# Projection tiles in order of need, earlier first mixers, weight loads on ScalarE's queue

## The reference

```python
# first kind, twice
z = rms_norm(x, g) @ w_in                      # 3612 columns: Fox, conv and NSA parts
o_a = fox_attention(fq, fk, fv, ff + fox_b) * silu(f_gate)
o_b = conformer_conv(glu_in, ...) * silu(c_gate)       # 31 taps, LayerNorm, pointwise
o_c = nsa_attention(nq, nkc, ..., cmp_v_w2) * silu(n_gate)  # compressed, selected, window
x = x + concat(o_a, o_b, o_c) @ w_out
# second kind, twice
z = rmsnorm(x, g1) @ w_in_2                    # gated delta net, differential attention,
                                               # sliding window attention, mLSTM
x = x + (sum over 4 branches of gate_b * (y_b @ w_branch[b])) @ w_out_2
x = x + square(relu(rmsnorm(x, g2) @ w_mlp1)) @ w_mlp2
```

## Time and profile before

| | us |
|---|---|
| median of 3 runs (3993.82 to 4000.56) | 3995.27 |
| the profiled execution | 3999.47 |
| its span, first to last instruction | 3997.7 |
| TensorE busy | 3478.4 (87%) |
| VectorE busy | 2067.8 (52%) |
| ScalarE busy | 1448.1 (36%) |
| GpSimd busy | 396.9 (10%) |

### The profile page before, as it was taken

One profiled execution on the slowest core, in us unless ns is written; L12 is line 12 of the kernel. 1 busy time (PEld: TensorE's weight loads), 2 busy tenths in 40 slices (PEclk: granted clock), 3 DMA queues, 4 the chain that ended last, 5 costly groups with the idle time before them and its releaser, 6 DMA issues. The chain is left out here.

```text
span 3997.7 us, 48121 instructions
## 1 busy us (share of the span) xinstructions
PE 3478.4 (87%) x17580; PEld 2861.8 (72%) x17580; DVE 2067.8 (52%) x4076; ACT 1448.1 (36%) x2809; POOL 396.9 (10%) x322
## 2 busy tenths in 40 slices
PE   7877888779789999779879999889999789689998
PEld 5766867568567888668657888668888577577886
DVE  3474634746328776445553333248875455563333
ACT  2313333134324444334334332225544344334322
POOL 0000000000002223000112111002222000112110
PEclk9987899889899999899979999889999899899999
DMA  4632046330244322422333333343321422433332
GB/s 137 175 96 72 20 115 180 98 75 20 70 129 132 88 82 64 115 65 63 94 93 92 95 95 94 102 120 106 96 79 61 116 70 68 112 90 86 93 95 84
DMA packets 570480, 373.52 MB, mean 93 GB/s; under 512 B 77020, under 2 KB 500956, under 8 KB 569980
## 3 DMA queue, kind: packets, MB, share of 16 engines
q1 hardware_dynamic: 570236, 370.33, 33.6%
HBM read 310.69 MB, written 59.57 MB: 93 GB/s over the span
## 5 line engine op out<-in xcount | busy, mean ns | idle before, releaser
L767 PE MATMUL bank<-h,w_hi 128*128 128x512 f32 x2240 | 974.0, 435 | 170.8 <-DVE w_low L760 91.3
L768 PE MATMUL bank<-h,w_hi 128*128 128x512 f32 x2240 | 913.4, 408 | 0.0
L769 PE MATMUL bank<-h,w_low 128*128 128x512 f32 x2240 | 910.9, 407 | 0.0
L754 ACT CAST w_hi<-w 128x1024 fp32r<-128x1024 f32 (+1 forms) x456 | 432.7, 951 | 699.9 <-DMA w<-in_w_mlp 398.7
L760 DVE TENSOR_TENSOR w_low<-w,w_hi 128x1024 fp32r<-128x1024 f32 (+1 forms) x456 | 514.3, 1128 | 289.2 <-ACT w_hi L754 281.2
L767 PEld LDWEIGHTS bank<-h,w_hi 128*128 128x128 f32 x2240 | 437.8, 195 | 302.5 <-DVE w_low L760 139.0
L769 PEld LDWEIGHTS bank<-h,w_low 128*128 128x128 f32 x2240 | 435.9, 195 | 110.2
L768 PEld LDWEIGHTS bank<-h,w_hi 128*128 128x128 f32 x2240 | 438.6, 196 | 104.3 <-issue 14.9
L768 PE MATMUL bank<-yT_low,w_hi 128*128 128x512 f32 x768 | 312.2, 407 | 0.0
L1423 ACT ACTIVATE prob<-bank,softmax_stat 128x512 f32<-128x512 f32 (+3 forms) x256 | 145.0, 568 | 300.8 <-DVE softmax_stat L1457 211.6
L1226 DVE TENSOR_TENSOR xT<-xT,bank 128x512 f32<-128x512 f32 x80 | 55.0, 687 | 285.4 <-PE bank L769 285.4
(11 more groups left out here) (409 smaller groups left out, 5744.0 us busy)
## 6 DMA issues: line engine op xcount, KB each, us to landing
w<-in_w_in SPq DMA_DIRECT2D x148, 512.0 KB, 4.2
w<-in_w_mlp SPq DMA_DIRECT2D x128, 512.0 KB, 4.0
w<-in_w_gate SPq DMA_DIRECT2D x64, 512.0 KB, 4.2
z<-z_tile SPq DMA_DIRECT2D x110, 256.0 KB, 4.3
w<-in_w_branch SPq DMA_DIRECT2D x64, 256.0 KB, 2.9
z_hi<-row_part_high SPq DMA_DIRECT2D x54, 256.0 KB, 2.0
z<-z_tile_low SPq DMA_DIRECT2D x54, 256.0 KB, 2.3
k_hi<-z_hi SPq DMA_DIRECT2D x36, 256.0 KB, 7.4
```

What stands on the lines that cost most here:

```text
L754: self.a.copy(self.wh[s][:, 0:d, 0:n], self.w[s][:, 0:d, 0:n]).then_inc(self.w_high.sem, 1)
L767: self.t.matmul(bank[0:n, :], wh, high, start=j == 0, stop=False)
L768: self.t.matmul(bank[0:n, :], wh, low, start=False, stop=False)
L769: return self.t.matmul(bank[0:n, :], wl, high, start=False, stop=j == self.depth(i) - 1)
```

## The change

- **Order.** A new function `sequence` gives the z tiles an order of their own; the rows of z in DRAM stay as they were. Layer one: ff first, then one tile each of fq, fk, fv, fg for the first pair of heads, the same for the second, then nq, glu, cg, nkc, nvc, nks, nkw, nvs, nvw, ng. Layer two: a_ab first, then q, k, v, z of each Gdn head in turn; from position 17 on as before. The waits for stored rows name the tile that is needed, head by head, in place of the last of the group.
- **Start.** Both layers go densely to unit 6 only. Layer one: Fox to unit 22, ConvAndCompress to unit 27, and Nsa runs beside the last two z tiles and the first `out` units. Layer two: Gdn to unit 47, and the gates of branch 3 are spread: three ahead of branch 0, two ahead of branch 1, three ahead of branch 2.
- **Pieces.** Fox 0.7 to 1.6 for each step and 2.0 to 4.0 at its end; a tap 0.75 to 0.2; Nsa 3.0 to 9.0 at its start; Gdn's first yield 1.0 to 5.0, 3.0 to 6.0 in head 0, 2.0 to 4.0 ahead of `o_normed`; Diff 2.0 to 6.0 and Mlstm 1.0 to 6.0 ahead of `h_normed`; Swa 0.95 to 1.15 for each step, and 1.0 to 2.0 twice.
- **Loads of the mixers.** Value rows first, then keys, then queries; gains and the like behind them; the rows of the second part as soon as their buffer is free. Semaphores are split to fit. In Gdn the scalars' loads come first. In Nsa the second keys, queries and the gates wait for their own tiles.
- **Weights.** `fetch` takes the engine; the first two loads are SyncE's, all others ScalarE's, ahead of `split_high` of the next unit.

```diff
+def sequence(first, last, groups):
+    order = []
+    for names in groups:
+        rows = [range(first[name] // P, last[name] + 1) for name in names]
+        order += [tile for part in zip(*rows, strict=True) for tile in part]
+    place = {tile: i for i, tile in enumerate(order)}
...
+ORDER1, PLACE1 = sequence(C1, LAST1, (("ff",), ("fq", "fk", "fv", "fg"), ("nq",), ("glu",), ("cg",), ("nkc",), ("nvc",), ("nks",), ("nkw",),
+                                      ("nvs",), ("nvw",), ("ng",)))
+ORDER2, PLACE2 = sequence(C2, LAST2, (("a_ab",), ("a_q", "a_k", "a_v", "a_z"), ("b_q",), ("b_k",), ("b_v",), ("c_q",), ("c_k",), ("c_v",),
+                                      ("d_q",), ("d_k",), ("d_v",), ("d_o",)))
...
-    def fetch(self, i):
+    def fetch(self, eng, i):
...
-                self.s.wait_ge(*self.multiplied(i - self.SLOTS))
+                eng.wait_ge(*self.multiplied(i - self.SLOTS))
...
+        self.units = [("z", 0, e) for e in ORDER2]
+        for s, early in enumerate(((0, 1, 2), (3, 4), (5, 6, 7))):
+            self.units += [("gate", 3, e) for e in early] + pairs[2 * KD * s:2 * KD * (s + 1)]
...
             if self.pieces(i) == 4:
                 yield
+                self.fetch(self.a, i + 2)
                 self.split_high(i + 1)
...
-        yield 3.0
+        yield 9.0
+        self.t.wait_ge(*self.stream.drained(self.stream.kept - 1))
         self.t.wait_ge(*self.gl_in(0))
...
-            stream.go_to(("z", 0, LAST1["fg"] + 2))
-            stream.until(("z", 0, LAST1["nvc"] + 3))
-            Fox(k, l, stream, w1).beside(stream, ("z", 0, LAST1["nvc"] + 2))
-            stream.until(("out", 0, 0))
-            ConvAndCompress(k, l, stream, kcmp, vcmp, table, w1).beside(stream, ("out", 0, 0), stream.forms_out)
+            stream.go_to(stream.units[PLACE1["fg", 0] + 2])
+            stream.until(stream.units[PLACE1["nvc", 0] + 2])
+            Fox(k, l, stream, w1).beside(stream, stream.units[PLACE1["nvc", 0] + 2])
+            stream.until(stream.units[PLACE1["ng", 2]])
+            ConvAndCompress(k, l, stream, kcmp, vcmp, table, w1).beside(stream, stream.units[PLACE1["ng", 2]], stream.forms_out)
...
-        yield 3.0
+        yield 3.0 if h else 6.0
...
+        start, scalars = self.prepare_sp(0), self.scalars_sp()
+        next(scalars)
         next(start)
...
+            yield (1.0 if n else 5.0) if share is None else share
...
+        self.stream.wait_stored(s, PLACE2["b_v", 3])
+        self.fetch_v(0)
+        self.fetch_k(0)
+        self.fetch_q(0)
...
-            yield 1.0
+            yield 6.0
             self.t.wait_ge(*self.h_normed(p))
...
-        stream.go_to(("z", 0, LAST2["a_ab"] + 2))
-        stream.until(("gate", 0, 0))
-        Gdn(k, l, stream).beside(stream, ("gate", 3, 2), stream.forms_out)
+        stream.go_to(stream.units[PLACE2["a_z", 0] + 2])
+        stream.until(("gate", 3, 0))
+        Gdn(k, l, stream).beside(stream, ("gate", 3, 0), stream.forms_out)
...
-    stream.until(("gate", 1, 0))
-    Diff(k, l, stream).beside(stream, ("gate", 1, 0))
-    stream.until(("gate", 2, 0))
-    Swa(k, l, stream).beside(stream, ("gate", 2, 0))
+    stream.until(("gate", 3, 3))
+    Diff(k, l, stream).beside(stream, ("gate", 3, 3))
+    stream.until(("gate", 3, 5))
+    Swa(k, l, stream).beside(stream, ("gate", 3, 5))
```

More of the change, by code:

```diff
@@ L72 @@
                                ("raw", 1.0, [("d_o", 512)])))
+def sequence(first, last, groups):
[4 more added lines that the diff above has]
+    place = {tile: i for i, tile in enumerate(order)}
+    return order, {(name, j): place[first[name] // P + j] for name in first for j in range(last[name] + 1 - first[name] // P)}
+ORDER1, PLACE1 = sequence(C1, LAST1, (("ff",), ("fq", "fk", "fv", "fg"), ("nq",), ("glu",), ("cg",), ("nkc",), ("nvc",), ("nks",), ("nkw",),
+                                      ("nvs",), ("nvw",), ("ng",)))
+ORDER2, PLACE2 = sequence(C2, LAST2, (("a_ab",), ("a_q", "a_k", "a_v", "a_z"), ("b_q",), ("b_k",), ("b_v",), ("c_q",), ("c_k",), ("c_v",),
+                                      ("d_q",), ("d_k",), ("d_v",), ("d_o",)))
 LEVELS = 7
@@ L726, in store_row @@
     def store_row(self, i):
-        if 0 <= i < self.kept:
+        if 0 <= i and self.units[i][0] == "z":
             e, n = self.units[i][2], self.width(i)
@@ L783, in __init__ @@
         self.l = l
-        self.units = [("z", 0, e) for e in range(len(TILES1))] + [("out", s, e) for s in range(2) for e in range(KD)]
+        self.units = [("z", 0, e) for e in ORDER1] + [("out", s, e) for s in range(2) for e in range(KD)]
         self.tiles, self.kept = TILES1, len(TILES1)
@@ L1035, in bank_of, with wait_kept @@
         return self.banks[i % 2]
+    def wait_kept(self, eng, i, last):
+        eng.wait_ge(*self.row_out[i].nth(sum(r % 3 == i and r <= last for r in self.kept_rows) - 1))
     def wait_row_free(self, eng, r):
@@ L1040, in wait_row_free @@
             return
[L1041 to L1044, removed]
+        if r - 3 in self.kept_rows:
+            self.wait_kept(eng, r % 3, r - 3)
+            return
+        kind, s, e = next(u for u, n in self.row.items() if n == r - 3 and u[0] == "branch")
+        if s == 0:
             eng.wait_ge(*self.done(self.at[kind, s, e]))
@@ L3470, in sp @@
[L3470 to L3475 removed]
+            self.fetch_maxima(p)
+            if p == 0:
+                self.fetch_rows(p)
+            for n in range(2 + 4 + 12 + 2):
+                if p == 0 and n == 6:
+                    for h in range(2):
+                        s.wait_ge(*self.v_turned(p, h))
+                        s.wait_ge(*self.o_turned(p, h))
+                    self.fetch_values(1)
+                if p == 0 and n == 2 + 4 + 8:
+                    s.wait_ge(*self.qk_made(p, 1, NT - 1))
+                    self.fetch_rows(1)
+                yield
@@ new lines, in fetch_values, with fetch_maxima @@
+    def fetch_values(self, p):
+        for h in range(2):
+            for x, name, landed in ((self.vf, "d_v", self.v_in), (self.of, "d_o", self.o_in)):
+                at = C2[name] + p * 256 + h * P
+                self.s.dma_start(x[h][:, :], self.k.z2[at:at + P, :]).then_inc(landed[h].sem, 16)
+    def fetch_maxima(self, p):
+        for d in range(2):
+            for h in range(2):
+                self.s.dma_start(self.pR[:, d, h, :], self.k.row(2 * p + 4 * d + h, self.k.rows_R)).then_inc(self.R_in.sem, 16)
```

201 lines of the change are left out of this document (109 added, 92 removed).

## The result

| | before | after |
|---|---|---|
| median of 4 runs each, us | 3995.2 | 3891.5 (3884.2 to 3900.1) |
| ratio, 95% interval | | 0.9739 (0.9716 to 0.9762) |
| profiled span, us | 3997.7 | 3891.8 |
| TensorE busy / idle in it, us | 3478.4 / 519.3 | 3469.6 / 422.2 |

The change wins 104 us where 220 were forecast; the time lies inside the range of the prediction, but close to rival C's (3906). The page of the kernel after: busy time and share of each engine, the split of the weights' low halves (it answers to the second line of the earlier trace rows), and the two DMA queues.

What follows compares the result with a forecast made beforehand. Bound: the mixers' chains of dependent steps, too little covered by stream pieces, with TensorE idle 519 us. Terms: 2 x (76 + 27 + 4 + 12) - 18 = 220 us, giving 3775 from the median; range 3700 to 3950.

Steps and rivals of the forecast that it cites:

- rival C: Landing and VectorE bind: stage starts gain nothing, rope tiles cost 20 us, convolution loses 18; 3906 us, chance 0.23.
- the queue: Layer two's weight loads on ScalarE's queue no longer stand behind mixer loads: 10.5 us in Diff, 2 in Mlstm a pass.
- rope tiles: Gdn in layer two: 8 more rope tiles on VectorE cost between 0 and 24 us a pass; 6 taken.
- Layer one's part: Layer one, a pass: Nsa wins 8 us, Fox 8, ConvAndCompress loses 12, sum 4, plus 12 of clock.
- ScalarE's issues: Whole run: 456 weight loads at 0.39 us are 178 us more for ScalarE; a tenth, 18 us, charged.
- Clock of layer one: Nsa granted 0.83 over 195 us; long gap cut and dense work out of the convolution give 12 us a pass.
- A piece moved to a place without a gap moves its 1.39 us too.: All stages: moving a stream piece to a gapless place wins nothing, so only changes of idle time were summed.
- Fox: Layer one: Fox's weights no longer stand behind its loads; 8 of its 10.8 us idle won a pass.
- Waits that cover ends: Layer two, more pieces ahead of waits: o_sum 10 us, y_tok of Diff 10.8, y_tok of Mlstm 14 a pass.
- Starts of Diff and Swa: Layer two: queries and keys land 16 and 13.5 us after the stage begins; won 2.0 in Diff, 2.5 in Swa.
- the rule against it: A second issuer saves only its own issue time; the queue's 12.5 us return as later queries and keys, total 186.
- rival E: Mixers: ScalarE's weight loads hold the softmax chain; 0.9 us a load cancels the gain, 1.2 gives 4064; chance 0.11.

Runs made afterwards that it cites:

- e3: The kernel before with only the issuer of the weights changed to ScalarE, and some semaphores split to fit; 3965.3 us.
- e6: e1 with only Nsa's new load order and 9 pieces in place of 3 at its start; 3833.3 us.
- e11: e6 with only the limit between Fox and ConvAndCompress moved from unit 19 to 24, so 20 pieces a pass go to Fox; 3876.3 us.
- e1: The changed kernel with layer one's tile order, limits, pieces and load order put back, weights still on ScalarE's queue; 3850.0 us.
- e8: e1 with the pieces at layer two's waits put back to what they were before the change, orders of tiles and loads still new; 3913.5 us.
- e7: e1 with 5 more pieces ahead of Diff's first transposes and 6 more ahead of Swa's, taken from their loops; 3825.8 us.

## Why the prediction missed half

Two steps of the sum failed. Layer one's part was forecast to win 32 us and cost 42: its clock was to give back 12 us a pass "with the long gap cut, and dense work out of the convolution", and it was taking dense work out of the convolution that lowered the clock. Layer two's waits were right in kind and summed too high, 206 us with their clock where 127 came: a wait that goes was counted whole, and the next-latest step took part of it. The measured time lies near rival C's 3906, and that is luck: C has nothing won by the queue, which alone won 32 us (e3), rope tiles at 20 us a pass, where 9.5 came, and layer one's clock gaining as in the forecast.

The forecast's 220 us were 160 of idle time and 78 of clock less 18 for ScalarE. The spans show 106: 97 of idle time and 9 of busy time. The missing 114 by terms:

| | forecast | measured | missing |
|---|---|---|---|
| idle time, layers of the second kind | 152 | 98 | 54 |
| their clock | 54 | 29 | 25 |
| idle time, layers of the first kind | 8 | -1 | 9 |
| their clock | 24 | -20 | 44 |
| ScalarE's issues | -18 | not seen | -18 |

- **Clock of layer one: wrong in sign, 44 us.** The step said that with the long gap cut and dense work out of the convolution 12 us a pass come back. Cutting Nsa's gap gave back 4.7 (e6, clock 0.93 in Nsa). Dense work out of the convolution did the reverse: its mean clock fell from 0.86 to 0.73, and Nsa's stayed at 0.83. In e11, where only pieces move, the layers of the first kind are busy 30 us longer than in e6 for the same records.
- **"A piece moved to a place without a gap moves its 1.39 us too."** This held for Fox, and the idle time of the convolution grew by 10 us as forecast (12), and it got 15 us shorter (17 forecast). So the idle time that the pieces leave behind was in the sum. What was not in it is the clock of the place that they leave: by lengths, 28 us of pieces taken away shortened the convolution by 14, of which 9 are idle time and the rest clock (e11 against e6). The sign of layer one's part was wrong: +32 forecast, -32 to -41 measured by the totals.
- **Fox.** 8 us of 10.8 were taken; its idle time fell from 22.8 to 20.8 (18.6 in e1, which has the queue without layer one's part). The wait for low halves stands at its dense start, up to 13.2 us before and 11.7 after, which no edit touches. I had placed it in the mixer.
- **Waits that cover ends: right.** o_sum, y_tok and AT fell as counted. Covered gaps in layer two gave back 0.5 us of clock for each us (e8), more than the 0.35 taken.
- **Starts of Diff and Swa: seen, and underpriced.** The prediction had the queries land 16 and 13.5 us after the stage begins, and named the waits on q_stacked as a sign to look for. They came, 7.4 and 8.6 us, and pieces could cover most of them (e7). Idle time a pass fell by 10.9 in Diff (23.3 summed), 4.5 in Swa (8.3), 22.5 in Mlstm (33), 7.9 in Gdn (11.5).
- **What is late next.** Where several steps of a chain were near one another, the next took part of the gain: prob 6.8 us in six waits in Diff, w_low 12.8 in six in Mlstm (4.3 before). In Diff prob grew by 5.5 us and 4.9 of the 11.6 for low halves are left; in Mlstm w_low took back 8.5 of the 15.0 that y_tok lost. Each is too short to show ahead in a list of waits. In e8 against e1, 40 us of named waits a pass were 19 us of idle time. Rope rows in Gdn cost 9.5 (2.3 to 11.8) where 6 was taken.
- **The queue.** 12.5 a pass were summed for it in layer two, 34 us with its clock; alone it is worth 32 us in all. That these agree is luck: 19 of the 32 fall in the layers of the first kind, where the forecast has only Fox's 8 a pass for it, and 13 in those of the second. There the value rows came later, as the rule against it has it.
- **ScalarE (rival E).** Excluded by e3: with 452 loads issued by ScalarE the kernel is faster, not slower. A cost as small as the 18 us in the sum is not excluded; no run separates it from what the queue wins.

## What to carry to other kernels

Before taking filler work from a stage, look at how long the stage would be without it: beside a long chain on another engine, filler is free, and it is paid for where it is put. A start that waits for several loads should have filler for the last of them, not for the first. Count a removed wait only up to the next-latest step of its chain. And where filler leaves, look for the clock too: here it cost more than the idle time.

## What the runs showed of the hardware

**The lower clock can outlast its gap while the engine is busy.** TensorE in the changed kernel, from the end of the 13.7 us wait in the convolution, and a later stretch in Nsa; then the stretch of e6 with the same matmuls of Nsa as the second:

```profile
227.40:254.00 26.60, 26.60 (x125) 26.60 (x126) 10.79 (x19) 0.27 (x1) 0.00 (x0) 0.50 0.01 1
...
408.00:442.00 34.00, 27.98 (x114) 24.85 (x113) 13.81 (x33) 6.58 (x18) 0.00 (x0) 0.51 0.03 8
```

```profile
401.70:424.00 22.30, 18.57 (x113) 15.96 (x113) 13.06 (x31) 5.71 (x17) 0.00 (x0) 0.85 0.01 4
```

For 26.6 us without any gap, in the compression's matmuls of 62 columns, the granted clock stayed at its lower level, 1.2 GHz. In Nsa of the changed kernel it was there from about 409 to 442 us at over 80% busy, with no gap of over 2.6 us in it; e6 did the same matmuls in 22 us. The Trainium skill, "TensorE: Matmul & The Clock Gate", section "HAM oscillation — how this bites in real kernels", lays low clock to idle gaps. Before the first stretch such a gap stands, but being busy again did not end the low clock. Before the second the clock was full up to 408 us, and no wait in the 10 us ahead of that was longer than 1.5 us. What brought it down there, and what ended either stretch, no run here tells apart.

**Clock is not a function of idle time.** e11 idles 412.9 us and e1 415.9, and yet e11 is busy 27.7 us longer for the same work. Idle time saved in one place says little of the clock in another; a gain in clock has to be looked for where it is to come.
